# A stick-breaking attention layer whose input arrives transposed, with the token scale multiplied in after the projections

## The chip, the core and the metric

The kernel runs as one program on one core of a Trainium2 chip. The metric is the device time of one execution in microseconds; lower is better. The kernel before takes 697.34 us (median of 3 runs, 697.03 to 698.51).

The engines are named as in the profile: PE is TensorE, PEld its weight loads, DVE VectorE, ACT ScalarE, POOL GpSimd, SP SyncE (which here only starts transfers).

## The reference

With DEPTH = 1 only layer 0 is computed: a pre-norm, stick-breaking attention with a SiLU gate, a residual, and a final norm. x is 1024 tokens by 1024 features, float32.

```
h = x * rsqrt(mean(x*x, -1) + eps) * norm_g         # per token scale, per feature gain
q, k, v, gate = split(h @ w_in, 4)                  # 1024 x 4096, 16 heads of 64
z = q k^T / 8, masked to key < query                # per head
log_beta = log_sigmoid(z); log_1m = log_beta - z
a = exp(log_beta + sum of log_1m over later keys)
o = a v;  y = x + (o * silu(gate)) @ w_out
out = y * rsqrt(mean(y*y, -1) + eps) * final_g
```

## The kernel before

Every matrix product is made in three float32r products of high and low parts (hi times hi, hi times lo, lo times hi). `hT` holds h by features: hi and lo, 8 feature blocks of 128, 1024 tokens. `half` 0 and 1 are tokens 0 to 511 and 512 to 1023. A weight unit is the 1024 x 128 slice of w_in for one kind (k, v, q or gate) and one pair of heads; one unit on one half is 24 matmuls of 128x512 into one PSUM bank.

The order of work is written out by hand, one in-order stream for each engine, with semaphores between them.

**The prologue.** x is loaded by tokens, in 8 blocks of 128 tokens (512 KB each). ACT and DVE sum the squares of each block, a root and one Newton step give `rstd` (one number for each token), and DVE and ACT multiply the blocks by it (`scale_x`). PE then transposes the scaled blocks into PSUM (`transpose_x`, 16 times four 128x128 transposes), ACT writes the hi part with the gain (`hi_x`), DVE the lo part (`lo_x`). Among them stand the six projections that pair 0 needs, in the order k0, v0, k1, v1, q0, q1 (kind and half), in two PSUM banks. ACT evicts each bank to the buffer `stage` (`to_stage`, a copy); DVE splits k and q into heads (`heads_hi`, `heads_lo`); v is transposed by PE and split. `z` below is the first scores matmul, the end of the prologue.

**The pairs.** Eight pairs of heads follow (p = 0 to 7), 16 slots each (s = 0 to 15, eight query blocks of rising width, 128 to 1024 keys, for each head). In a slot PE makes the scores of this query block into `z_ps`, half of a projection for the next pair into the one bank `proj_ps`, the products of a with v for the slot before, and the transposes of a. ACT makes two sigmoids from the scores (`rest` and the beta values). DVE runs the scan over `rest` (L1016), whose length is the width of the block. POOL multiplies beta by the scanned row (L1115), makes the lo parts of the weights (L1091) and multiplies o by the gate (L1103). `evac_at` puts one eviction of `proj_ps` at the head of every even slot: k in slots 2 and 4, v in 6 and 8, q in 10 and 12, the gate in 14 and in slot 0 of the next pair. ACT does it before. PE's next projection waits for it (one bank), and in slots 6 and 8 so do PE's transposes of v (L495).

**The last pair and the tail.** Pair 7 has only gate projections (evicted in slots 0, 4 and 8), beside them the output projection begins; then come the output projection, the residual and the final norm.

## Time and profile before

| | us |
|---|---|
| median of 3 runs | 697.34 |
| the profiled execution, its own time | 696.88 |
| its span | 694.8 |
| PE busy | 670.2 (96%) |
| DVE busy | 481.4 (69%) |
| ACT busy | 426.4 (61%) |
| POOL busy | 282.0 (41%) |

The time of the profiled execution is 2.1 us more than its span. A row of the timeline gives the start, the duration, the engine, the line and operation, the output and inputs, how many instructions are merged in it, and in square brackets how long the engine had been idle before it and who ended that.

### The profile page before, as it was taken

The numbers are of one execution on the slowest core, as the hardware profiler recorded it, in microseconds if no ns is written. First come the engines' busy times: TensorE is split into PE (matmuls) and PEld (weight loads), VectorE is DVE, ScalarE is ACT, GpSimd is POOL, SyncE is SP. The second block draws the span as 40 slices with busy tenths as digits, with TensorE's granted clock in tenths as the row PEclk, the third lists the DMA queues.
The fourth block names the chain that finished last, engine by engine and source line by source line (L and its number), as shares of the span: only waits on it lengthen the run. The fifth ranks groups of instructions, "written<-read, shape, count | busy, mean of one in ns | idle before, by whom it ended". The sixth has DMA issues, their size and how long they took to land.

```text
span 694.8 us, 10872 instructions
## 1 busy us (share of the span) xinstructions
PE 670.2 (96%) x3426; PEld 563.4 (81%) x3426; DVE 481.4 (69%) x636; ACT 426.4 (61%) x795; POOL 282.0 (41%) x225
## 2 busy tenths in 40 slices
PE   5999999999999999999999999999999997999995
PEld 4787888888888888888888888888888776888884
DVE  5835666776678677867776677667766798735565
ACT  5614767676767676767676767666766675622333
POOL 2122434453545445444554454435353543315100
PEclk9999999999999999999999999999999999999999
DMA  7131301241114110410042014201420148523332
GB/s 288 46 95 43 92 31 31 61 122 33 31 51 131 31 33 33 136 44 20 25 129 67 16 32 121 76 15 30 121 60 30 61 137 290 211 92 94 125 145 92
DMA packets 28122, 57.64 MB, mean 83 GB/s; under 512 B 3376, under 2 KB 3376, under 8 KB 28080
## 3 DMA queue, kind: packets, MB, share of 16 engines
q1 hardware_dynamic: 25312, 51.13, 24.0%
q10 hardware_dynamic: 2736, 6.03, 2.3%
q8 instruction: 16, 0.26, 0.2%
q14 instruction: 26, 0.21, 0.1%
q0 software_dynamic: 32, 0.00, 0.0%
HBM read 37.23 MB, written 11.53 MB: 70 GB/s over the span
## 4 chain that ended last, share of the span: by engine, by line
PE 90%; DVE 5%; ACT 2%; DMA 1%; POOL 1%; issue 1%; ACTq 0%; DVEq 0%; POOLq 0%
PE proj_ps L486 46%; PE o_ps L632 10%; PE z_ps L581 9%; PE t_ps L644 9%; PE z_ps L561 8%; PE proj_ps L561 4%; PE o_ps L486 2%; DVE rest L1016 2%; PE t_ps L495 1%; DMA a_group<-x 1%; DVE gate L982 1%; ACT stage L719 1%; PE z_ps L506 1%; DVE arena L314 0%; DVE aT L1000 0%
## 5 line engine op out<-in xcount | busy, mean ns | idle before, releaser
L486 PE MATMUL proj_ps<-hT,w_split 128*128 128x512 f32 x1464 | 359.9, 394 | 2.2 <-DVE hT L889 1.4
L486 PEld LDWEIGHTS proj_ps<-hT,w_split 128*128 128x128 f32 x1464 | 270.0, 188 | 57.6 <-DVE hT L889 2.3
L1115 POOL TENSOR_TENSOR a_group<-a_group,rest 128x128 f32<-128x128 f32 (+7 forms) x128 | 158.0, 1235 | 300.0 <-DVE rest L1016 300.0
L1016 DVE TENSOR_TENSOR_SCAN rest<-rest,restart 128x128 f32<-128x128 f32 (+7 forms) x128 | 203.6, 1591 | 16.0 <-ACT rest L809 15.5
L1000 DVE TENSOR_TENSOR aT<-t_ps,aT 128x512 fp32r<-128x512 f32 (+2 forms) x160 | 93.1, 607 | 35.1 <-ACT aT L794 33.6
L794 ACT ACTIVATE aT<-t_ps 128x512 fp32r<-128x512 f32 (+2 forms) x160 | 80.2, 532 | 59.2 <-PE t_ps L644 57.6
L1091 POOL TENSOR_TENSOR w_split<-w_raw,w_split 128x512 fp32r<-128x512 f32 x64 | 91.7, 1434 | 38.1 <-DVE w_split L851 38.1
L581 PE MATMUL z_ps<-arena 128*128 128x512 f32 (+2 forms) x384 | 96.3, 366 | 0.3 <-DVE arena L938 0.3
L938 DVE TENSOR_TENSOR arena<-stage,arena 64x512 fp32r<-64x512 f32 x64 | 44.0, 687 | 67.9 <-ACT arena L739 67.3
L809 ACT ACTIVATE rest<-z_ps 128x128 f32<-128x128 f32 (+7 forms) x128 | 83.9, 655 | 8.9 <-PE z_ps L581 8.6
L644 PE MATMUL t_ps<-ident,a_group 128*128 128x128 f32 x576 | 84.6, 274 | 0.4 <-POOL a_group L1115 0.4
L811 ACT ACTIVATE a_group<-z_ps 128x128 f32<-128x128 f32 (+7 forms) x128 | 84.4, 659 | 0.0
L632 PE MATMUL o_ps<-aT,arena 128*128 128x512 f32 (+2 forms) x320 | 82.7, 364 | 1.7 <-DVE aT L1000 1.7
L644 PEld LDWEIGHTS t_ps<-ident,a_group 128*128 128x128 f32 x576 | 70.0, 142 | 8.5 <-issue 0.6
L719 ACT ACTIVATE stage<-proj_ps 128x512 f32<-128x512 f32 x61 | 36.5, 598 | 61.3 <-PE proj_ps L486 61.3
L632 PEld LDWEIGHTS o_ps<-aT,arena 128*128 128x128 f32 x320 | 59.5, 188 | 16.6 <-DVE aT L1000 4.2
L581 PEld LDWEIGHTS z_ps<-arena 128*128 128x128 f32 x384 | 59.6, 190 | 5.2 <-DVE arena L938 0.8
L561 PE MATMUL z_ps<-arena,hT 128*128 128x512 f32 x246 | 57.7, 391 | 0.0
L786 ACT ACTIVATE oT<-o_ps 64x512 f32<-64x512 f32 x32 | 19.0, 593 | 62.2 <-PE o_ps L632 62.2
L561 PEld LDWEIGHTS z_ps<-arena,hT 128*128 128x128 f32 x246 | 45.8, 188 | 9.4
L990 DVE TENSOR_TENSOR oT<-o_ps,oT 64x512 f32<-64x512 f32 x32 | 22.0, 689 | 25.6 <-ACT oT L786 25.3
L746 ACT ACTIVATE w_split<-w_raw 128x512 fp32r<-128x512 f32 x56 | 35.9, 641 | 0.6
(86 smaller groups left out, 460.7 us busy)
## 6 DMA issues: line engine op xcount, KB each, us to landing
w_raw<-w_in SPq DMA_DIRECT2D x64, 256.0 KB, 2.6
arena<-arena SPq DMA_DIRECT2D x32, 256.0 KB, 4.3
wo_raw<-w_out SPq DMA_DIRECT2D x16, 256.0 KB, 3.8
o_hi_scratch<-o_split SPq DMA_DIRECT2D x14, 256.0 KB, 2.1
o_lo_scratch<-o_split SPq DMA_DIRECT2D x14, 256.0 KB, 2.4
hT<-o_hi_scratch SPq DMA_DIRECT2D x14, 256.0 KB, 4.9
hT<-o_lo_scratch SPq DMA_DIRECT2D x14, 256.0 KB, 6.0
a_group<-x SPq DMA_DIRECT2D x14, 256.0 KB, 3.6
```

The lines of the kernel that those rows point to most:

```text
L486: mm = nc.tensor.matmul(bank[:, :], w_split[:, ring, wl, b, :], hT[:, hl, b, half * HALF:(half + 1) * HALF], start=(b == 0 and n == 0), st ...
L561: mm = nc.tensor.matmul(bank[:, :], hT[:, ol, b, tokens], w_out_of(nh, wl)[:, b, :], start=(b == first and m == 0), stop=(b == last and m ...
L581: mm = nc.tensor.matmul(z[:, c0:c1], q, k_of(par, hh, swapped)[:, c0 - first:c1 - first], start=not swapped, stop=swapped)
L632: mm = nc.tensor.matmul(o_ps[:, c:HALF], v_of(apar)[:, j, 2 * ahh:2 * ahh + 2, :] .rearrange("p x d -> p (x d)"), moving, start=(j == 0 an ...
L644: last = nc.tensor.transpose(t_ps[t % 2][:, i2 * P:(i2 + 1) * P], a_g[grp][:, i2, j * P:(j + 1) * P], ident[:, :])
L794: nc.scalar.activation(to, t_ps[t % 2][:, rel * P:HALF], ACT.Copy).then_inc(t_hi, 1)
L809: nc.scalar.activation(rest[:, s % 2, S - width:S], z_ps[s % 2][:, first:first + width], ACT.Sigmoid, scale=-SCALE).then_inc(rest_ready, 1)
L811: nc.scalar.activation(a_g[grp][:, i % GQ, 0:width], z_ps[s % 2][:, first:first + width], ACT.Sigmoid, scale=SCALE).then_inc(beta_ready, 1)
L1000: nc.vector.tensor_tensor(lo, t_ps[t % 2][:, rel * P:HALF], hi.bitcast(F32), ALU.subtract).then_inc(t_lo, 1)
L1016: nc.vector.tensor_tensor_scan(span, span, restart[:, S - 1:(S - 1 - width if width < S else None):-1], 0.0, ALU.mult, ALU.max).then_inc(s ...
L1091: nc.gpsimd.tensor_tensor(to[:, 1], w_raw[:, part, :].rearrange("p (b n) -> p b n", b=4), to[:, 0].bitcast(F32), ALU.subtract).then_inc(w_ ...
L1115: nc.gpsimd.tensor_tensor(a, a, rest[:, s % 2, S + 1 - width:S + 1], ALU.mult).then_inc(a_ready, 1)
```

## The change

x is handed to the kernel a second time, by features (`x_t`, transposed on the host), and loaded in 16 tiles of 128 features by 512 tokens. ACT and DVE split each tile into hi and lo with the gain, straight from SBUF and without the token scale. The token scale commutes with the projection, so it is multiplied in when a projection is evicted: `to_stage` is now DVE's, one tensor_tensor of the PSUM bank with `token_scale`, a 128x1024 tile that has the scale of each token in all partitions. To make it, ACT squares the 16 tiles, POOL adds the squares over the 8 feature blocks of each half (7 adds for each half, 128x512), PE sums them over the partitions with a column of ones, the root and the Newton step follow as before, PE transposes the broadcast result, and ACT copies it to SBUF. DVE, not POOL, makes the lo parts of the first four weight tiles. The prologue's projections have six banks instead of two; the warm-up is 12 transposes instead of 34. The a matrix is stored as a triangle to make room, and the residual's x tiles go to other buffers.

```diff
@@ buffers
+        token_scale = sb("token_scale", [P, S])
+        ones = sb("ones", [P, 1])
+        def x_raw(n):
+            return x_cols[:, n // KB, n % KB, :]
+        squares = [oT[:, 0:HALF], oT[:, HALF:S], gate[:, 0:HALF], gate[:, HALF:S]]
+        first_banks = [proj_ps, o_ps] + z_banks
@@ PE
-            def transpose_x(n):
-                half, b = n // KB, n % KB
-                wait(pe, xt_lo, n - 3)
-                for i in range(4):
-                    ...
-                last.then_inc(xt_done, 1)
+            def sum_squares(half):
+                pe.wait_ge(squares_added, (KB - 1) * (half + 1))
+                for i in range(GQ):
+                    last = nc.tensor.matmul(t_ps[half][:, i:i + 1], rest[:, half, i * P:(i + 1) * P], ones[:, :],
+                                            start=True, stop=True)
+                last.then_inc(ssq_done, 1)
+            def spread_scale(half):
+                pe.wait_ge(rstd_ready, 5 * half + 5)
+                ...
+                    last = nc.tensor.transpose(t_ps[half][:, i * P:(i + 1) * P],
+                                               rstd[:, b:b + 1].to_broadcast([P, P]), ident[:, :])
             for h, (kind, half) in enumerate(PROLOGUE):
                 unit = "kvq".index(kind)
-                wait(pe, stage_ready, h - 1)
+                if h == 4:
+                    transpose_v(0, 0, 1, 1)
                 for b in range(KB):
                     pe.wait_ge(xt_lo, KB * half + b + 1)
                     pe.wait_ge(w_ready, 2 * unit + b // 4 + 1)
-                    mm = project(unit % 2, (proj_ps, o_ps)[h % 2], half, b)
+                    mm = project(unit % 2, first_banks[h], half, b)
+                    if b == 3 and h == 2:
+                        spread_scale(0)
+                    if b == 3 and h == 3:
+                        sum_squares(1)
+                if h == 1:
+                    sum_squares(0)
+                if h == 3:
+                    spread_scale(1)
@@ ACT
+HI_THEN_SQUARES = (0, 0, 1, 0, 1, 0, 1, 4, 0, 1, 0, 1, 0, 1, 0, 1)
+            for n in range(2 * KB):
+                hi_x(n)
+                for _ in range(HI_THEN_SQUARES[n]):
+                    square_x(squared)
+                    squared += 1
+                if n == KB + 4:
+                    root(slice(0, GQ), t_ps[0][:, 0:GQ], ssq_done, 1)
+            scale_half(0)
+            while squared < 2 * KB:
+                ...
-            def to_stage(bank, h, buf):
-                act.wait_ge(proj_done, h + 1)
-                nc.scalar.activation(stage[:, buf, :], bank[:, :], ACT.Copy).then_inc(stage_ready, 1)
@@ DVE
-                nc.vector.scalar_tensor_tensor(hT[:, 1, b, cols], z_banks[n % 4][:, :], g_col[:, b:b + 1],
+                nc.vector.scalar_tensor_tensor(hT[:, 1, b, cols], x_raw(n), g_col[:, b:b + 1],
                                                hT[:, 0, b, cols].bitcast(F32), ALU.mult, ALU.subtract
+            def to_stage(bank, h, half, buf):
+                dve.wait_ge(proj_done, h + 1)
+                nc.vector.tensor_tensor(stage[:, buf, :], bank[:, :], token_scale[:, half * HALF:(half + 1) * HALF],
+                                        ALU.mult).then_inc(stage_ready, 1)
@@ DVE, slot()
                 if evac:
                     kind, half, h = evac
+                    ...
+                    to_stage(proj_ps, h, half, half)
@@ POOL
-            for n in range(2 * UNITS0 + 2):
+            for half in range(2):
+                for b in range(1, KB):
+                    add_square(half, b)
+            for n in range(4, 2 * UNITS0 + 2):
                 lo_w(n, (n // 2) % 2, n % 2)
```

The first of three places is DVE in slots 5 to 8 of pair 0, before; the later pairs have the same order, with the split of o (`o_split`) in slots 2 and 6 besides. The scan is listed as SCALAR_TENSOR_TENSOR on `rest`; its width tells the slot.

```order
L1016 SCALAR_TENSOR_TENSOR rest<-rest,restart 128x768 [waits rest_ready]
L1000 TENSOR_TENSOR aT<-t_ps,aT 128x384 [waits t_hi]
L1016 SCALAR_TENSOR_TENSOR rest<-rest,restart 128x896 [waits rest_ready]
L945 TENSOR_TENSOR arena<-t_ps,arena 128x4x128 [waits t_hi]
L1000 TENSOR_TENSOR aT<-t_ps,aT 128x256 [waits t_hi]
L1016 SCALAR_TENSOR_TENSOR rest<-rest,restart 128x1024 [waits rest_ready]
L1000 TENSOR_TENSOR aT_pad<-t_ps,aT_pad 128x128 [waits t_hi]
```

The same place after:

```order
L1022 SCALAR_TENSOR_TENSOR rest<-rest,restart 128x768 [waits rest_ready]
L917 TENSOR_TENSOR stage<-proj_ps,token_scale 128x512 [waits proj_done,qk_split]
L1006 TENSOR_TENSOR aT<-t_ps,aT 128x384 [waits t_hi]
L1022 SCALAR_TENSOR_TENSOR rest<-rest,restart 128x896 [waits rest_ready]
L902 TENSOR_TENSOR arena<-t_ps,arena 128x4x128 [waits t_hi]
L1006 TENSOR_TENSOR aT<-t_ps,aT 128x256 [waits t_hi]
L1022 SCALAR_TENSOR_TENSOR rest<-rest,restart 128x1024 [waits rest_ready]
L917 TENSOR_TENSOR stage<-proj_ps,token_scale 128x512 [waits proj_done,qk_split]
L1006 TENSOR_TENSOR aT_pad<-t_ps,aT_pad 128x128 [waits t_hi]
```

Both evictions of v now stand on DVE behind the scan of the slot before.

The second place is DVE in the prologue after, up to the first eviction; `hT<-x_cols` is `lo_x`, `w_split` rows are the split of the weights.

```order
L851 CAST w_split<-w_raw 128x512 [waits w_loaded0,g_loaded]
L911 TENSOR_TENSOR w_split<-w_raw,w_split 128x512 [waits w_hi]
L879 SCALAR_TENSOR_TENSOR hT<-x_cols,g_col,hT 128x512 [waits xt_hi] x3
L851 CAST w_split<-w_raw 128x512 [waits w_loaded1]
L911 TENSOR_TENSOR w_split<-w_raw,w_split 128x512 [waits w_hi]
L879 SCALAR_TENSOR_TENSOR hT<-x_cols,g_col,hT 128x512 [waits xt_hi] x5
L851 CAST w_split<-w_raw 128x512 [waits w_loaded0]
L911 TENSOR_TENSOR w_split<-w_raw,w_split 128x512 [waits w_hi]
```

All of these read SBUF only; before, `lo_x` read `z_ps`, and POOL did the subtraction for the weights.

The third place is PE around the sum of squares after: the end of v0 (bank `o_ps`), the four sums, and the start of k1.

```order
L499 MATMUL o_ps<-hT,w_split 128x512 x2
L517 MATMUL t_ps<-ones,rest 128x1 [waits squares_added]
L517 MATMUL t_ps<-ones,rest 128x1 x3
L499 MATMUL z_ps<-hT,w_split 128x512 [waits w_ready,xt_lo]
L499 MATMUL z_ps<-hT,w_split 128x512 x2
```

PE's projections of k1 stand behind a wait for POOL's first seven adds; the same four sums stand again in the middle of v1, behind a wait for all fourteen.

## Rows read from the trace of the kernel before

**Rows 1.** The page: busy time of each engine, and the chain by engine.

```profile
PE 670.2 (96%) x3426; PEld 563.4 (81%) x3426; DVE 481.4 (69%) x636; ACT 426.4 (61%) x795; POOL 282.0 (41%) x225
PE 90%; DVE 5%; ACT 2%; DMA 1%; POOL 1%; issue 1%; ACTq 0%; DVEq 0%; POOLq 0%
```

**Rows 2.** Windows: us, busy by engine, PEclk (granted clock), DMA share, GB/s.

```profile
200.00:271.00 71.00, 71.00 (x371) 60.21 (x371) 50.98 (x59) 48.60 (x91) 33.54 (x27) 1.00 0.20 61
...
580.00:584.00 4.00, 3.68 (x15) 3.45 (x16) 3.07 (x7) 2.33 (x6) 0.71 (x1) 0.59 0.96 298
```

**Rows 3.** Groups by line, 0 to 60 us; columns as on the page.

```profile
L1091 POOL TENSOR_TENSOR w_split<-w_raw,w_split 128x512 fp32r<-128x512 f32 x8 | 10.4, 1314 | 38.1 <-DVE w_split L851 38.1
L506 PE MATMUL z_ps<-ident,a_group 128*128 128x128 f32 x48 | 7.8, 274 | 0.5 <-DVE a_group L882 0.3
```

**Rows 4.** Timeline of the prologue.

```profile
4.13 0.20 ACT L671 ACTIVATE newton<-eps_col 128x1 f32<-128x1 f32 x1
...
5.54 1.23 DVE L877 CUSTOM_DVE_ANT_0 gate<-a_group 128x1024 f32<-128x1024 f32 x1 [4.38 <-DMA a_group<-x]
...
9.62 0.30 ACT L667 ACTIVATE rstd<-ssq,eps_col 128x4 f32<-128x4 f32 x1
...
10.83 0.16 DVE L868 TENSOR_TENSOR rstd<-rstd,newton 128x4 f32<-128x4 f32 x1
...
50.56 5.74 PE L486 MATMUL o_ps<-hT,w_split 128*128 128x512 f32 x24
...
59.36 0.73 PE L581 MATMUL z_ps<-arena 128*128 128x256 f32 x4 [0.34 <-DVE arena L938]
```

**Rows 5.** Timeline, slots 5 to 8 of pair 5.

```profile
429.13 2.75 DVE L1016 TENSOR_TENSOR_SCAN rest<-rest,restart 128x768 f32<-128x768 f32 x1
...
432.43 0.60 PE L495 MATMUL t_ps<-ident,stage 128*128 128x128 f32 x4
...
437.30 1.78 POOL L1115 TENSOR_TENSOR a_group<-a_group,rest 128x896 f32<-128x896 f32 x1 [2.02 <-DVE rest L1016]
...
437.66 0.41 DVE L1000 TENSOR_TENSOR aT<-t_ps,aT 128x256 fp32r<-128x256 f32 x1
438.38 2.85 DVE L1016 TENSOR_TENSOR_SCAN rest<-rest,restart 128x1024 f32<-128x1024 f32 x1 [0.31 <-ACT rest L809]
...
440.03 0.60 ACT L719 ACTIVATE stage<-proj_ps 128x512 f32<-128x512 f32 x1 [0.78 <-PE proj_ps L486]
...
440.69 0.66 PE L495 MATMUL t_ps<-ident,stage 128*128 128x128 f32 x4
```

**Rows 6.** Timeline, slot 15 and the next pair's slot 0: scan, PE's next projection.

```profile
473.59 2.29 DVE L1016 TENSOR_TENSOR_SCAN rest<-rest,restart 128x1024 f32<-128x1024 f32 x1 [1.08 <-ACT rest L809]
...
475.93 3.03 PE L486 MATMUL proj_ps<-hT,w_split 128*128 128x512 f32 x12
```

**Rows 7.** Timeline, POOL and DVE right after that.

```profile
476.03 2.00 POOL L1115 TENSOR_TENSOR a_group<-a_group,rest 128x1024 f32<-128x1024 f32 x1 [2.33 <-DVE rest L1016]
...
476.65 1.93 DVE L982 TENSOR_TENSOR gate<-stage,gate 128x512 f32<-128x512 f32 x1 [0.77 <-ACT gate L776]
...
477.98 1.74 POOL L1091 TENSOR_TENSOR w_split<-w_raw,w_split 128x512 fp32r<-128x512 f32 x1
...
478.70 1.30 DVE L1016 TENSOR_TENSOR_SCAN rest<-rest,restart 128x128 f32<-128x128 f32 x1
```

**Rows 8.** Timeline, slot 2 of pair 5: splits on ACT and DVE.

```profile
413.00 1.27 ACT L739 ACTIVATE arena<-stage 64x512 fp32r<-64x512 f32 x2
...
414.30 1.39 DVE L938 TENSOR_TENSOR arena<-stage,arena 64x512 fp32r<-64x512 f32 x2 [2.24 <-ACT arena L739]
...
415.72 1.29 DVE L1000 TENSOR_TENSOR aT<-t_ps,aT 128x512 fp32r<-128x512 f32 x2
...
416.93 0.68 DVE L1006 TENSOR_TENSOR o_split<-oT,o_split 128x512 fp32r<-128x512 f32 x1
```

**Rows 9.** Timeline, PE in the last pair.

```profile
580.32 0.79 PE L632 MATMUL o_ps<-aT_pad,arena 128*128 128x256 f32 x2 [4.16 <-DVE aT_pad L1000]
```

More of the change, by code:

```diff
@@ L378, in _ @@
                 load_w(n, n % 2, n % 2, kinds[n // 2] * KB)
-                if n == 1:
-                    for b in (5, 7):
+                if n < 2:
+                    for b in range(4 * n + 1, 4 * n + 5, 2):
+                        load_x_block(sp, b)
+                if n == 3:
+                    for b in range(KB, 2 * KB):
                         load_x_block(sp, b)
@@ L660, in _, with root @@
         def _(act):
+            act.dma_start(g_col[:, :], norm_g).then_inc(g_loaded, 16)
             for b in range(0, KB, 2):
                 load_x_block(act, b)
-            act.wait_ge(consts_ready, 2)
-            def root(cols, ready, count):
+            act.wait_ge(eps_ready, 1)
+            def root(cols, sums, ready, count):
                 act.wait_ge(ready, count)
-                nc.scalar.activation(rstd[:, cols], ssq[:, cols], ACT.Sqrt, scale=1.0 / D,
+                nc.scalar.activation(rstd[:, cols], sums, ACT.Sqrt, scale=1.0 / D,
@@ L688, in _, with scale_half @@
-            act.wait_ge(x_squared_dve, 2)
-            root(slice(0, 4), x_squared, 2)
-            square_x(2, 4)
-            def scale_x(blocks):
-                for b in blocks:
-                    nc.scalar.activation(x_blocks[b], x_blocks[b], ACT.Copy, scale=rstd[:, b:b + 1]
-                                         ).then_inc(x_scaled_act, 1)
-            act.wait_ge(rstd_ready, 5)
-            scale_x(X_ACT[:1])
+            def scale_half(half):
+                act.wait_ge(scale_done, half + 1)
+                nc.scalar.activation(token_scale[:, half * HALF:(half + 1) * HALF], t_ps[half][:, :], ACT.Copy
+                                     ).then_inc(scale_ready, 1)
@@ L738, in heads_hi @@
                     to = q_of(par, hh) if kind == "q" else k_of(par, hh, False)
-                    last = nc.scalar.activation(to[rows, cols], stage[rows, half, :], ACT.Copy)
+                    last = nc.scalar.activation(to[rows, cols], stage[rows, buf, :], ACT.Copy)
                 last.then_inc(qk_hi, 1)
+            for h, (kind, half) in enumerate(PROLOGUE):
+                if kind in "kq":
+                    act.wait_ge(stage_ready, h + 1)
+                    heads_hi(kind, 0, half, 0 if kind == "k" else half)
+                if h == 0:
+                    root(slice(GQ, KB), t_ps[1][:, 0:GQ], ssq_done, 2)
+                    scale_half(1)
+                if h in (3, 5):
+                    v_hi(0, h // 2 - 1, h // 2 - 1, h // 2 - 1)
             def split_hi_w(ring, part, unit):
@@ L950, in _, with split_w @@
+            def split_w(n):
+                next_w(n)
+                lo_w(n)
+            dve.wait_ge(g_loaded, 16)
+            split_w(0)
+            for n in range(KB):
+                lo_x(n)
+                if n == 2:
+                    split_w(1)
+            split_w(2)
+            split_w(3)
             for n in range(KB, 2 * KB):
+                if n == KB + 5:
+                    dve.wait_ge(table_loaded, 1)
+                    dve.wait_ge(root_ready, 1)
+                    rsqrt(slice(0, GQ), t_ps[0][:, 0:GQ], 0)
@@ new lines, in _ @@
+                if h in (3, 5):
+                    dve.wait_ge(t_done, h // 2)
+                to_stage(first_banks[h], h, half, h % 2)
+                if kind in "kq":
+                    heads_lo(kind, 0, half, h % 2, {0: 1, 2: 2, 4: 3, 5: 4}[h])
+                if h == 1:
+                    for n in (4, 5):
+                        dve.wait_ge(proj_done, 3)
+                        next_w(n)
+                    dve.wait_ge(root_ready, 2)
+                    rsqrt(slice(GQ, KB), t_ps[1][:, 0:GQ], 1)
@@ L1092, in lo_w, with add_square @@
                                         to[:, 0].bitcast(F32), ALU.subtract).then_inc(w_ready, 1)
-            for n in range(2 * UNITS0 + 2):
+            def add_square(half, b):
+                n = KB * half + b
+                pool.wait_ge(x_squared, n + 1)
+                total = rest[:, half, 0:HALF]
+                other = squares[(n - 1) % 4] if b == 1 else total
+                if b > 1:
+                    pool.wait_ge(squares_added, (KB - 1) * half + b - 1)
+                nc.gpsimd.tensor_tensor(total, other, squares[n % 4], ALU.add).then_inc(squares_added, 1)
+            for half in range(2):
+                for b in range(1, KB):
+                    add_square(half, b)
+            for n in range(4, 2 * UNITS0 + 2):
                 lo_w(n, (n // 2) % 2, n % 2)
```

219 lines of the change are left out of this document (78 added, 141 removed).

## The prediction

> **What bounds the kernel now.** I read the page first: PE is busy 96% of the span and carries 90% of the chain that ended last [rows 1]. The windows then say where it is not: a pair in the middle has PE busy for all of its 71 us, with DVE at 51, ACT at 49 and POOL at 34 [rows 2]. So a microsecond taken from PE is a gain, and a microsecond by which another engine lets PE wait is a loss, for in the middle nothing gives it back. Last I read the timeline at two places: the prologue, which ends at 59.36 us with the first scores matmul [rows 4], and the slots in which `proj_ps` is evicted [rows 5, 6].
>
> **The change removes** 64 transposes of 128x128 from PE in the prologue: 48 take 7.8 us [rows 3], so 64 take 10.4 us. It also removes the order "squares, root, scale, transpose, split" ahead of the first projection. Were PE the only limit, the prologue would be about 10 us shorter.
>
> **What now sets the prologue.** One rule of this machine decides it, and the trace shows it. A DVE instruction with two inputs in SBUF and a POOL instruction with inputs in SBUF do not run together. POOL's L1115 runs 476.03 to 478.03; DVE's gate product, asked for at 476.65, ends at 478.58, 0.55 us after POOL. POOL's L1091, asked for at 477.98, ends at 479.72, 1.14 us after DVE; and the short scan, asked for at 478.70, ends 0.28 us after that [rows 7]. They wait in full, and take turns. A DVE instruction with one input in PSUM doesn't wait: the 256-wide L1000 takes 0.41 us in the middle of POOL's L1115 [rows 5]. The Trainium skill says the same in "SBUF — State Buffer" (section "SBUF: two separate sides": the port pair of the two is an exclusive lock held for a whole instruction), and by it the change is worse than its list of operations. Were it a sharing of bandwidth, the first rival's sum below would hold.
>
> Before, `lo_x` read PSUM. Now it reads two SBUF tiles while POOL adds squares. Step by step, all times from the span's start:
>
> - First data: two 512 KB blocks had landed by 5.54 us [rows 4]; the first tile and the first weights are half of that and are there by about 4.2 (an estimate from that row). ACT was free at 4.33 [rows 4] and now issues one more transfer (some 0.5 us): first hi ends at 5.5, first lo at 6.2, and PE starts there. ACT's order puts the second square at 9.2, and POOL's first add runs 9.2 to 10.5 (1.31 us each alone [rows 3]).
> - From there DVE and POOL take turns, 0.54 + 1.17 = 1.7 us each time [rows 7], where DVE alone would take 0.68 [rows 8]. Five `lo_x` and four adds: the last tile of half 0 is ready at 10.5 + 5 x 0.54 + 4 x 1.17 = 17.9. Then the third weight tile (two DVE steps, with adds 6 and 7 between them) at 21.0, the fourth at 22.0. k0 ends at 18.6, v0 (24 matmuls, 5.5 us by 5.74 with the last one's tail [rows 4]) at 26.5, the four sums at 26.9.
> - Root and Newton step take 1.4 us (9.62 to 10.99 [rows 4]): 28.4. The remaining `lo_x` and the adds 8 to 14 follow in turns, with two head splits of k0 among them: 29.05 + 5 x 1.17 + 2 x 1.29 + 2 x 0.54 + 2 x 0.58 = 39.7.
> - PE has k1 done at 33.2, half of v1 at 35.95, and waits there for add 14: 39.8, a wait of 3.8 us. Then the sums 0.4, the second half 2.7, the scale's transposes 0.5, those of v 0.6: q0 starts at 44.0, q1 ends at 55.0. The lo weights of q (POOL, at 42.8) are just in time; so is the swap of k's halves, which is issued near 48.
> - After q1: transposes of v 0.6, eviction 0.6, head split 1.27 on ACT and 1.39 on DVE [rows 8]: `z` at 59.0. Before it is 59.36. The gain is 0.4 us where 10 were on offer.
>
> To this I add the clock. After PE had waited 4.16 us [rows 9], its granted clock was 0.59 in the next 4 us [rows 2], that is mostly the lower of its two levels, 1.2 GHz: (1 - 0.59) x 4 = 1.6 us lost. The new wait of 3.8 us is of that size. The Trainium skill ("TensorE: Matmul & The Clock Gate", Part 1) has the clock fall to half after idling, and the trace agrees. **Prologue: -0.4 + 1.6 = +1.2 us.** Its bounds are -9.5 (no turns) and +5 (below).
>
> **The eviction in the pairs.** 0.6 us leaves ACT, and about the same comes to DVE: reading a PSUM bank and one SBUF tile, the second of two L1000 adds 1.29 - 0.69 = 0.60 us [rows 8]. DVE has the time; what counts is where it stands in DVE's order, which is behind the scan of the slot before, and PE waits for it.
>
> - Slot 6: the scan of 768 ends at 431.88, the eviction at 432.48. PE's transposes of v run from 432.43, with their first load some 0.2 ahead [rows 5]: 0.3 us late.
> - Slot 8: the scan of 1024 ends at 441.23, the eviction would end at 441.83. ACT's ended at 440.63, and PE's transposes came at once [rows 5]. 1.2 us late. The 0.3 us of slot 6 come off, since this scan's end is set by POOL's L1115 (end 439.08, plus 2.15) and not by PE. Both slots: 1.2 us.
> - Slot 0: the scan ends at 475.88, the eviction at 476.48; PE's next projection stood at 475.93 [rows 6]. 0.6 us.
> - Slots 2, 4, 10, 12 and 14: the scan before is short or done before the projection is. In slot 2 DVE waited 2.24 us for ACT's head split [rows 8], so the eviction fits in that wait. Behind it, ACT's head split starts 0.1 us later, and PE isn't touched. Cost nothing; without that cover each would be 0.6.
>
> What queues behind the late eviction: on PE everything of the slot (it is in order); on ACT the head split or the sigmoid of the gate; on DVE nothing that wasn't waiting for PE anyhow. Since PE is busy all the time [rows 2], 1.8 us per pair stay. Pairs 1 to 6: 10.8. Pair 0 has no gating work on POOL ahead of its scans; I take one stall of 0.6. In the last pair DVE is itself late (PE waits 4.16 us for it [rows 9]), and two gate evictions of 0.6 stand in its chain: 1.2. **Pairs: +12.6 us.** Bounds: nothing, if PE were not held at these slots, and 16.5, if the scan of slot 15 too had a POOL instruction ahead of it as that of slot 7 has (0.56 more, 2.85 against 2.29 [rows 5, 6]), in seven pairs.
>
> The rest costs nothing: transfers of x for the residual go to other buffers at the same point of SP's queue, the triangle has the same rows for the same instructions, the 256 KB transfers replace the 512 KB ones, and the shorter warm-up lies ahead of the first data. SP now issues eight x tiles between the weights of v and of q, but they are wanted only from 14 us on.
>
> **Sum.** +1.2 + 12.6 = +13.8 us on the profiled execution's own 696.9 us gives 710.7. That execution is 0.5 us below the median of the three runs, so I write 711.
>
> **Rivals.**
> - *The turns don't hold in the prologue* (lock for this form of DVE instruction absent, or POOL gives way). For it: no row shows a scalar_tensor_tensor with both tiles in SBUF beside POOL. Against it: tensor_tensor and the scan both wait [rows 7]. Then half 0 is split at 12.5, v0 ends at 19.1, POOL's adds are back to back and end at 30.6, and `z` comes at 49.9: -9.5, no long wait and no clock loss. 696.9 - 9.5 + 12.6 = 700.
> - *The clock is low in k0 and v0 too.* For it: PE works only 0.7 of each 1.7 us there and then waits 2.4 us, and rows 2 show what a wait does. Against it: none of these gaps is as long as the wait of rows 9. v0 delays the sums, and by them everything to `z`: up to +3.7 us more, 715.
> - *Faster: PE is not held at slots 6, 8 and 0.* The place is DVE's queue at the eviction, the price the 11.4 us of pairs 0 to 6. It needs the wide scans to end before the projection does. For it: a scan without POOL ahead is 0.56 us shorter (2.29 against 2.85 [rows 5, 6]), and DVE's total has room [rows 2]. Against it: in slot 8 the scan starts when ACT's sigmoid ends [rows 5], and that starts with PE's scores, so even 2.29 us would end at 440.67 and the eviction 0.6 after ACT's. Then only the prologue and the last pair count: 696.9 + 1.2 + 1.2 = 699 with my prologue, 689 with the first rival's, and it is faster from the point where the prologue gives more than the pairs take. As one case I put it at 693.
> - *The change doesn't do what it says*: only where the eviction waits for `token_scale`; after the prologue that is set once and is no wait.
>
> **Chances.** My forecast 0.62 (706 to 715); no turns 0.15 (697 to 703); low clock in k0 and v0 0.12 (713 to 718); PE not held 0.11 (687 to 699). The range of 8 in 10 is 699 to 717: it takes in most of the second case and leaves out the last. What a measurement of this kernel can tell from no change is about 0.2%, 1.4 us. Faster by more than that: 0.11, from the last case and the lower edge of the second. Within it: 0.04. Slower: 0.85.
>
> **What would show it.** The first scores matmul at 59 to 61 us (50 would be the first rival). POOL's adds and DVE's `lo_x` alternating, with `lo_x` shown at 1.7 us instead of 0.7. PE waiting for POOL's last add near 36 to 40 us, with a granted clock well under 1 behind it. In each pair PE waiting for DVE's `stage` in slots 8 and 0, together 1.8 us, and each pair longer by that. DVE busy up by about 36 us in the pairs, ACT down by as much. If PE shows no waits in the middle, the forecast is wrong by 12 us; if `lo_x` stays at 0.7 us while POOL adds, it is wrong by 10.

## The result, and the profile after

| | before | after |
|---|---|---|
| median, us | 697.18 (696.77 to 698.51, 4 runs) | 716.06 (715.09 to 716.97, 4 runs) |
| span of the profiled execution | 694.8 | 715.2 |
| first scores matmul (`z`) | 59.36 | 64.84 |
| pair 0, from `z` to the end of its last scan | 63.14 | 64.96 |
| pairs 1 to 6, each | 70.67 | 72.77 |
| last pair | 61.82 | 62.58 |
| rest | 86.4 | 86.1 |

The change makes the kernel slower: ratio 1.0265 [1.0253, 1.0277]. A pair is measured here from the end of one scan of slot 15 to the next. The 20.4 us of span are 5.5 of the prologue, 1.8 of pair 0, 12.6 of pairs 1 to 6, 0.8 of the last, less 0.3.

The page of after, busy time and chain by engine, as [rows 1]:

```profile
PE 679.5 (95%) x3364; PEld 562.1 (79%) x3364; DVE 526.1 (74%) x686; ACT 394.8 (55%) x744; POOL 295.4 (41%) x234
PE 81%; DVE 7%; issue 5%; ACT 3%; POOL 2%; DMA 1%; DVEq 0%; ACTq 0%; POOLq 0%
```

PE has 62 instructions less than before and is busy 9.3 us longer; DVE gained 44.7 us, ACT lost 31.6. PE's share of the chain fell from 90% to 81%: it now waits. In a middle pair DVE is at 56.4 us where it was at 51.0, and ACT at 43.7 where it was at 48.4; over seven pairs that is 37 and 33 us, where about 36 was named for each.

The timeline of the prologue of after, filtered to DVE, then to POOL, then to PE (L879 is `lo_x`, L1106 POOL's add, L517 the sums over the partitions):

```profile
10.51 7.55 DVE L879 SCALAR_TENSOR_TENSOR hT<-x_cols,g_col,hT 128x512 fp32r<-128x512 f32 x5
...
23.23 3.39 DVE L879 SCALAR_TENSOR_TENSOR hT<-x_cols,g_col,hT 128x512 fp32r<-128x512 f32 x5
...
12.83 2.98 POOL L1106 TENSOR_TENSOR rest<-rest,gate 128x512 f32<-128x512 f32 x2 [0.43 <-ACT gate L700]
...
40.00 3.21 POOL L1106 TENSOR_TENSOR rest<-rest,gate 128x512 f32<-128x512 f32 x2
...
18.12 0.97 PE L499 MATMUL proj_ps<-hT,w_split 128*128 128x512 f32 x3 [0.74 <-DVE hT L879]
21.32 8.37 PE L499 MATMUL o_ps<-hT,w_split 128*128 128x512 f32 x24 [2.23 <-DVE w_split L911]
29.52 0.95 PE L517 MATMUL t_ps<-ones,rest 128*128 128x1 f32 x8
...
43.27 1.26 PE L517 MATMUL t_ps<-ones,rest 128*128 128x1 f32 x8 [2.18 <-POOL rest L1106]
...
64.84 0.74 PE L601 MATMUL z_ps<-arena 128*128 128x256 f32 x4 [0.77 <-DVE arena L895]
```

With POOL beside them five `lo_x` take 7.55 us; with POOL idle five take 3.39. But v0's 24 matmuls take 8.37 us where such 24 took 5.74 before [rows 4]. The windows say why (us, busy PE, PEld, DVE, ACT, POOL, granted clock, DMA):

```profile
15.00:20.00 5.00, 2.61 (x9) 1.17 (x8) 4.96 (x4) 4.40 (x8) 4.57 (x4) 1.00 0.81 284
20.00:25.00 5.00, 3.69 (x9) 2.94 (x10) 4.97 (x6) 0.33 (x1) 2.15 (x2) 0.51 0.26 81
25.00:30.00 5.00, 5.00 (x23) 4.06 (x21) 1.62 (x3) 0.00 (x0) 0.00 (x0) 0.81 0.07 27
...
40.00:45.00 5.00, 2.82 (x15) 2.19 (x14) 3.93 (x7) 0.26 (x1) 4.49 (x4) 0.90 0.00 0
45.00:50.00 5.00, 5.00 (x23) 4.13 (x22) 1.67 (x7) 0.60 (x1) 1.20 (x1) 0.76 0.41 105
```

PE was busy 2.6 of 5 us, and then its clock was 0.51, nearly all at 1.2 GHz. By the clock column 0.49 x 5 + 0.19 x 5 = 3.4 us are lost around v0, of which 2.6 show in v0's own 8.37 us, and 0.10 x 5 + 0.24 x 5 = 1.7 in v1.

The timeline of after, slots 6 and 8 of a middle pair and slot 0 of the last, as [rows 5, 6]; L917 is the eviction, L508 the transposes of v:

```profile
372.63 2.82 DVE L1022 TENSOR_TENSOR_SCAN rest<-rest,restart 128x768 f32<-128x768 f32 x1
...
375.38 0.66 DVE L917 TENSOR_TENSOR stage<-proj_ps,token_scale 128x512 f32<-128x512 f32 x1
...
376.09 0.66 PE L508 MATMUL t_ps<-ident,stage 128*128 128x128 f32 x4
...
382.16 2.63 DVE L1022 TENSOR_TENSOR_SCAN rest<-rest,restart 128x1024 f32<-128x1024 f32 x1 [0.52 <-ACT rest L809]
...
384.71 0.66 DVE L917 TENSOR_TENSOR stage<-proj_ps,token_scale 128x512 f32<-128x512 f32 x1
...
385.43 0.66 PE L508 MATMUL t_ps<-ident,stage 128*128 128x128 f32 x4 [0.75 <-DVE stage L917]
...
567.16 1.62 PE L499 MATMUL proj_ps<-hT,w_split 128*128 128x512 f32 x6 [0.49 <-DVE stage L917]
```

Each eviction starts when the scan ahead of it ends, and PE stands behind it. In slot 6 PE's transposes start at 376.09, right after the eviction's end at 376.04, and yet no idle time of PE is listed: the matmul before them was still running. Their weight load had waited 0.27 us for DVE's `stage`.

One thing was in no forecast. PE's projections of one pair, by windows filtered to `proj_ps` (busy PE, then clock), before and after:

```profile
193.00:263.63 70.63, 46.99 (x192) 1.00 0.20 61
```

```profile
202.50:275.20 72.70, 47.79 (x192) 1.00 0.20 59
```

The same 192 matmuls at the same clock take 0.80 us more. Taken over pairs 1 to 6, one starts 231.7 ns after the other before and 235.5 after, though the matmul and the sizes of its operands are the same.

### The profile page after: what moved, and what is told of

Same layout as the page of the kernel before. It is cut to its first block, busy times and chain, and to the rows that moved or that the text cites. A ratio compares the mean times of both kernels' runs of the same rounds, so it can differ in the third digit from the quotient of the medians.

```text
span 715.2 us, 10802 instructions
## 1 busy us (share of the span) xinstructions
PE 679.5 (95%) x3364; PEld 562.1 (79%) x3364; DVE 526.1 (74%) x686; ACT 394.8 (55%) x744; POOL 295.4 (41%) x234
## 4 chain that ended last, share of the span: by engine, by line
PE 81%; DVE 7%; issue 5%; ACT 3%; POOL 2%; DMA 1%; DVEq 0%; ACTq 0%; POOLq 0%
PE proj_ps L499 39%; PE o_ps L652 9%; PE t_ps L664 8%; PE z_ps L601 8%; PE z_ps L581 8%; PE proj_ps L581 4%; PE z_ps L499 2%; ACT rest L809 2%; DVE stage L917 2%; DVE rest L1022 2%; PE t_ps L508 1%; POOL rest L1106 1%; PE o_ps L499 1%; DVE hT L879 1%; DMA x_cols<-x_t 1%
## 5 line engine op out<-in xcount | busy, mean ns | idle before, releaser
L499 PEld LDWEIGHTS proj_ps<-hT,w_split 128*128 128x128 f32 x1416 | 262.8, 189 | 69.8 <-DVE hT L879 8.0
L1132 POOL TENSOR_TENSOR a_tri<-a_tri,rest 128x128 f32<-128x128 f32 (+7 forms) x128 | 156.7, 1225 | 313.8 <-DVE rest L1022 300.0
L1022 DVE TENSOR_TENSOR_SCAN rest<-rest,restart 128x128 f32<-128x128 f32 (+7 forms) x128 | 209.9, 1641 | 17.2 <-ACT rest L809 16.5
L1095 POOL TENSOR_TENSOR w_split<-w_raw,w_split 128x512 fp32r<-128x512 f32 x60 | 87.1, 1452 | 8.7 <-DVE w_split L851 8.7
L664 PE MATMUL t_ps<-ident,a_tri 128*128 128x128 f32 x576 | 84.5, 274 | 0.4 <-POOL a_tri L1132 0.4
L811 ACT ACTIVATE a_tri<-z_ps 128x128 f32<-128x128 f32 (+7 forms) x128 | 84.3, 659 | 0.0
L895 DVE TENSOR_TENSOR arena<-stage,arena 64x512 fp32r<-64x512 f32 x64 | 45.4, 710 | 43.2 <-ACT arena L740 42.8
L664 PEld LDWEIGHTS t_ps<-ident,a_tri 128*128 128x128 f32 x576 | 69.9, 141 | 8.3 <-issue 0.6
L740 ACT ACTIVATE arena<-stage 64x512 fp32r<-64x512 f32 x64 | 40.3, 630 | 64.1 <-DVE stage L917 63.7
L917 DVE TENSOR_TENSOR stage<-proj_ps,token_scale 128x512 f32<-128x512 f32 x59 | 40.1, 680 | 16.1 <-PE proj_ps L499 16.1
```

Of the source, the lines that this page charges most:

```text
L499: mm = nc.tensor.matmul(bank[:, :], w_split[:, ring, wl, b, :], hT[:, hl, b, half * HALF:(half + 1) * HALF], start=(b == 0 and n == 0), st ...
L664: last = nc.tensor.transpose(t_ps[t % 2][:, i2 * P:(i2 + 1) * P], a_of(GQ * grp + i2)[:, j * P:(j + 1) * P], ident[:, :])
L811: nc.scalar.activation(a_of(i), z_ps[s % 2][:, first:first + width], ACT.Sigmoid, scale=SCALE).then_inc(beta_ready, 1)
L1022: nc.vector.tensor_tensor_scan(span, span, restart[:, S - 1:(S - 1 - width if width < S else None):-1], 0.0, ALU.mult, ALU.max).then_inc(s ...
L1095: nc.gpsimd.tensor_tensor(to[:, 1], w_raw[:, part, :].rearrange("p (b n) -> p b n", b=4), to[:, 0].bitcast(F32), ALU.subtract).then_inc(w_ ...
L1132: nc.gpsimd.tensor_tensor(a, a, rest[:, s % 2, S + 1 - width:S + 1], ALU.mult).then_inc(a_ready, 1)
```

## The experiments

The sums below use three numbers of each profiled execution: `z`, the middle pair (mean of pairs 1 to 6), and the time.

| | us (median) | ratio to before | `z` | pair 0 | middle pair |
|---|---|---|---|---|---|
| e1_act_evicts | 707.59 | 1.0136 [1.0118, 1.0155] | 65.92 | 63.74 | 71.20 (one 72.45) |
| e2_before_dve_evicts | 708.19 | 1.0153 [1.0136, 1.0170] | 59.42 | 63.90 | 72.39 |
| e3_thin_adds | 703.29 | 1.0081 [1.0064, 1.0097] | 52.34 | 64.95 | 72.77 |
| e4_layout | 713.16 | 1.0213 [1.0192, 1.0234] | 64.61 | 63.96 | 72.38 |
| e5_dve_adds | 709.75 | 1.0179 [1.0162, 1.0196] | 55.77 | 66.47 | 72.79 |
| e6_v_unscaled | 709.77 | 1.0175 [1.0158, 1.0192] | 60.95 | 63.97 | 71.70 |
| e7_room32 | 717.85 | 1.0291 [1.0274, 1.0308] | 62.86 | 65.04 | 72.87 |
| e8_warm | 712.88 | 1.0217 [1.0200, 1.0235] | 61.13 | 64.95 | 72.76 |
| e9_w_place | 712.24 | 1.0218 [1.0197, 1.0238] | 59.50 | 63.95 | 72.43 |
| e10_best | 699.24 | 1.0020 [1.0008, 1.0032] | 55.59 | 65.95 | 71.30 |
| e11_best_gate | 701.60 | 1.0054 [1.0038, 1.0070] | 57.58 | 63.38 | 71.26 (one 72.58) |
| e12_best_order | 698.54 | 1.0026 [1.0000, 1.0051] | 52.91 | 64.94 | 71.23 (one 76.31) |

The prologues of e1, e4, e6, e7 and e9 have the changed kernel's instructions in its order (e6 leaves the token factor out of two evictions of v; e4, e7 and e9 have tensors at other places), and yet their `z` differ by 6.4 us. With it goes the granted clock. In e6 and e9 it is 1.00 in every 5 us up to 55 us; here is e6 where after had 0.51, and then e9 there and in the 5 us before:

```profile
20.00:25.00 5.00, 3.47 (x15) 2.87 (x16) 4.96 (x6) 0.00 (x0) 2.38 (x2) 1.00 0.26 55
```

```profile
15.00:20.00 5.00, 1.93 (x6) 0.97 (x6) 4.97 (x4) 3.85 (x7) 4.42 (x5) 1.00 0.69 245
20.00:25.00 5.00, 4.48 (x20) 3.76 (x21) 4.97 (x7) 0.00 (x0) 1.51 (x1) 1.00 0.36 105
```

In e9 PE was busy for less of the 5 us than in after (1.93 against 2.61), and its clock did not fall. The timed runs show the same spread: the mean granted clock of e9's four was 0.994, 0.991, 0.986 and 0.986, and their times 708.7, 710.9, 713.9 and 713.6. All four of after were between 0.986 and 0.989. So `z` of one execution has a spread of its own, and the middle pair is the safer number.

### Eviction and layout, two by two

```diff
@@ e1: ACT, slot()
+                    act.wait_ge(proj_done, h + 1)
+                    nc.scalar.activation(stage[:, half, :], proj_ps[:, :], ACT.Copy).then_inc(stage_ready, 1)
@@ e2: DVE, slot() of the kernel before
+                    dve.wait_ge(proj_done, h + 1)
+                    nc.vector.tensor_scalar(stage[:, half, :], proj_ps[:, :], 1.0, None, ALU.mult
+                                            ).then_inc(stage_ready, 1)
@@ e4
-        ones = sb("ones", [P, 1])
+        ones = sb("ones", [P, HALF])[:, 0:1]
```

> The changed kernel with the evictions of the pairs back on ACT, as a plain copy (the token factor is left out of all projections of the pairs; the prologue is as changed). Theory: the 14.9 us that the pairs lost are PE's waits for DVE's late eviction in slots 6, 8 and 0, about 1.25 us per pair, plus a second term of 0.8 us per pair that I had not forecast, a projection matmul taking 235.3 ns from start to start instead of 231.1. If that second term also comes from DVE's eviction, all of it goes: pitch 231, pairs of 70.65 us, z still at 64.8, time about 701. If it comes from where the tensors now lie in SBUF, only the waits go: pitch 235, pairs of 71.5, time about 707. If neither theory holds and the pairs lose their time elsewhere, it stays near 716.

> The kernel before with one edit: the evictions of the pairs are moved from ACT to DVE, at the place in DVE's order that they have in the changed kernel (multiplied by the constant 1.0, so nothing is left out). Prologue and tensors stay as before. Theory of the late eviction: PE waits about 1.25 us per pair for DVE's stage. With the slower matmuls caused by DVE's eviction: pitch 235, pairs of 72.8, time 697.2 + 14 = 711. With the slower matmuls caused by the tensors' places: pitch 231, pairs of 72.0, 697.2 + 9 = 706. If eviction by DVE costs nothing and the pairs lost their time otherwise: 697.

> The changed kernel with one tensor made larger: the one-column tile of ones gets 512 columns of room, of which only the first is used. With that rest, aT, stage, w_split and all the tensors behind it in SBUF lie at exactly the addresses that they have in the kernel before, instead of 2044 bytes lower. If the 4 ns of each projection matmul come from the place of the weights (w_split) in SBUF: pitch back to 231, 0.8 us less in each pair, time about 709 to 710. If they come from DVE's eviction: pitch 235, time 716.

PE's waits in e2 (us in total, times, longest):

```profile
PE t_ps L495 <- DVE stage L975: 5.8, 7, 0.9
PE proj_ps L486 <- DVE stage L975: 4.2, 9, 0.6
```

PE busy with `proj_ps` in one middle pair, of e1, of e2 and of e4:

```profile
200.75:271.95 71.20, 47.76 (x192) 1.00 0.20 60
```

```profile
195.60:268.00 72.40, 47.04 (x192) 1.00 0.21 59
```

```profile
200.80:273.20 72.40, 47.00 (x192) 1.00 0.21 59
```

The middle pair is 70.67 us (ACT evicts, old places), 72.39 and 72.38 (DVE evicts, old places: e2 and e4), 71.20 (ACT, new places), 72.77 (DVE, new places). Late eviction costs 1.72 us at the old places and 1.57 at the new; the places cost 0.53 and 0.39. The slower matmuls follow the places and not the eviction. e4's pair fell by 0.39 us where 0.8 was named, and its time was 3 us above 709 to 710: the projections came back to 231.7 ns and PE spent 0.79 us less of a pair on them, but the 512-wide matmuls of aT went from 229.5 to 234.6 ns (0.24 us more with `o_ps`), and PE, busy 71.02 us of the pair and not 71.62, was idle 0.2 us longer. e2 came out 2 us above its 706 because a pair lost 1.72 and not 1.25: I had added up the waits that the trace lists, and such a one as in slot 6 above is not among them.

### Which tensor it is

```diff
@@ e7 (8) and e9 (504), ahead of w_split
         eps_col = sb("eps_col", [P, 1])
+        sb("room", [P, 8])
```

> The changed kernel with 32 bytes of unused room ahead of w_split, and nothing else. In the kernel before, w_split began at a multiple of 64 bytes in SBUF and aT 32 bytes off one; in the changed kernel it is the other way round. From start to start a projection matmul (weights from w_split) took 231.7 ns before and 235.5 after, a matmul of aT against v 234.6 before and 229.5 after. Theory: a tensor that begins 32 bytes off a multiple of 64 makes PE's reads of it slower. Then the projection matmuls take 231.7 again and those of aT stay at 229.5: 192 x 3.8 ns = 0.7 us less per pair, pairs of 72.05, 710 to 711 in all. If it is the distance from other tensors, or the 2016 bytes by which w_split moved, the projection stays at 235.5 and the time at 716.

> The changed kernel with 2016 bytes of unused room ahead of w_split, so that w_split alone lies again where it lay before; every other tensor stays where the change put it. Moving it by 32 bytes left the projection matmuls at 235.7 ns from start to start; moving it together with all tensors behind the ones by 2016 bytes gave 231.7, and slowed the matmuls of aT from 229.5 to 234.6. Theory one, it is w_split's own place that counts for the projection: 231.7 for it, 229.5 still for aT, pairs of 72.05 us, 710 to 711. Theory two, it is the place of another tensor that moved (rest, aT, stage, the identity) or the distance to it: 235.5 for the projection, 716.

PE busy with `proj_ps` in one middle pair, e7, then e9:

```profile
200.70:273.50 72.80, 47.83 (x192) 1.00 0.21 59
```

```profile
195.70:268.10 72.40, 47.05 (x192) 1.00 0.20 59
```

e7's theory falls: moved by 32 bytes, the projection stays at 235.7 ns from start to start. In e9 w_split alone is back at its old place, and it is 232.0. So w_split's place sets it (only `wo_raw`, which shares its room and which PE never reads, moved with it). But the 512-wide matmuls of aT, which did not move in either, went from 229.5 to 232.3 in e7 and to 235.0 in e9. A pair of e9 was 72.43 us and not the 72.05 that was named, and its time 712.24 and not 710 to 711. What in w_split's address does this stays open; no rule is shown, only that three addresses give three pairs of figures.

### The prologue

```diff
@@ e3: POOL
-                nc.gpsimd.tensor_tensor(total, other, squares[n % 4], ALU.add)
+                nc.gpsimd.tensor_tensor(total[:, 0:8], other[:, 0:8], squares[n % 4][:, 0:8], ALU.add)
@@ e8: PE
+                    if h == 0:
+                        keep_warm(5)
                     pe.wait_ge(xt_lo, KB * half + b + 1)
@@ e5: the adds on DVE
+                nc.vector.tensor_tensor(total, other, squares[n % 4], ALU.add).then_inc(squares_added, 1)
```

> The changed kernel with POOL's 14 adds of squares cut from 512 to 8 columns, in the same order and with the same waits (the sum of squares is left out for all but 8 columns). Theory of the turns: lo_x falls from 1.2 to 1.5 us to 0.68 everywhere, half 0 is split by about 14 us instead of 18, PE waits neither for POOL nor long for DVE, and z comes at 52 to 54 instead of 64.84: time about 716 - 11 = 705. If the turns cost little and the prologue is held by the landing of x or by the low clock: z at 62 or later, 713 to 716. The pairs stay at 72.8 us either way.

> The changed kernel with identity transposes of no use put where PE waits in the prologue: 5 ahead of each feature tile of k0, 18 ahead of v0, 16 ahead of the second sum of squares (0.11 us each at full clock). Theory: part of the late z is the clock. In the changed kernel it was at half for about 6.8 us in k0 and v0 and 3.4 us in the second half of v1, 5 us of loss. If work without use keeps it up, these go: z at 60 to 62, time 711 to 713. If the turns alone set the chain (PE's low clock being hidden by its waits for the next tile), z stays at 64 to 65; and if the transposes come in the way of the tiles, z is at 66 or later.

> The changed kernel with the 14 adds of squares moved from POOL to DVE, after all of lo_x, and the order of the prologue behind them arranged to fit (ACT makes hi of all 16 tiles first; the sums and the spreading of the token factor come one half projection later on PE; v0's eviction goes ahead of k0's head split). Nothing is left out. Theory of the turns: with POOL out of the way lo_x takes 0.68 us, PE never waits long in the prologue, its clock stays at full, and the adds (14 x 0.67 = 9.4 us) fit into DVE's free time after 20 us: z at 49 to 53 instead of 64.8, time 701 to 704. If DVE is too full behind 25 us, the late evictions move z to 56 or more, and 708 or more. If adds of two SBUF tiles on DVE held ACT or PE up as well, z would be near 60.

The timeline of e3, `lo_x` and PE's first projections:

```profile
10.46 2.74 DVE L879 SCALAR_TENSOR_TENSOR hT<-x_cols,g_col,hT 128x512 fp32r<-128x512 f32 x4
...
7.73 8.55 PE L499 MATMUL proj_ps<-hT,w_split 128*128 128x512 f32 x24 [3.37 <-DVE hT L879]
16.11 5.76 PE L499 MATMUL o_ps<-hT,w_split 128*128 128x512 f32 x24
```

e3 shows the turns: with POOL's adds shortened and nothing else taken from DVE, `lo_x` is at 0.68 us from start to start again, k0 (once its tiles are there) and v0 run through, and `z` is 12.5 us earlier, all at full clock. Its median is 12.8 us below that of after. e8 shows the clock apart from the turns: its `lo_x` mean is that of after (1202 ns both, 748 in e3), and its v0 took 5.85 us and not 8.37. Here is the group of `lo_x` in e8, and from its timeline v0:

```profile
L888 DVE SCALAR_TENSOR_TENSOR hT<-x_cols,g_col,hT 128x512 fp32r<-128x512 f32 x16 | 18.4, 1202 | 2.5 <-ACT hT L714 2.5
```

```profile
21.67 5.85 PE L499 MATMUL o_ps<-hT,w_split 128*128 128x512 f32 x24
```

`z` is 3.7 us earlier than in after, and all four timed runs had a mean clock of 0.991 to 0.994, where after's had 0.986 to 0.989. e6 and e9 come to the same or lower without filling (60.95 and 59.50), but only in some executions. The turns at full clock cost the rest: 61.1 less 52.3, 8.8 us, or 7.2 by e9. e5 removes the turns without leaving anything out, but has its q0 and q1 chain in series at the end. PE waited there (timeline), and the clock was 0.66 in the next window:

```profile
55.77 1.12 PE L600 MATMUL z_ps<-arena 128*128 128x256 f32 x4 [4.36 <-DVE arena L895]
```

```profile
55.00:60.00 5.00, 4.23 (x14) 3.52 (x15) 2.47 (x5) 2.92 (x6) 1.18 (x2) 0.66 0.08 31
```

So `z` missed its 49 to 53 by 2.8 us, pair 0 took 1.5 us more, and the time missed 701 to 704 by 6.

### One place of the late eviction

```diff
@@ e6: ACT evicts v unscaled; its factor goes into the split of aT
-                    nc.scalar.activation(to, t_ps[t % 2][:, rel * P:HALF], ACT.Copy).then_inc(t_hi, 1)
+                    nc.scalar.activation(to, t_ps[t % 2][:, rel * P:HALF], ACT.Copy,
+                                         scale=rstd[:, j:j + 1]).then_inc(t_hi, 1)
```

> The changed kernel with v's evictions in the pairs back on ACT as plain copies, and v's token factor multiplied in elsewhere: at the split of the transposed weights aT, whose partitions are v's tokens, as the per-partition scale of ACT's copy and of DVE's subtraction. The number of instructions stays as it is; nothing is left out. Theory of the late eviction, place by place: PE's waits for DVE's stage in slots 6 and 8 (the transposes of v) go, that of slot 0 stays: 1.2 us less per pair, pairs of 71.5 to 71.6, 707 to 708 in all. If the loss came from DVE's added work as such and not from these two places, only the 1.3 us of DVE time would count: 714. If the scaled forms take longer than the plain ones on ACT or DVE (0.1 us each, 24 per pair), it gives part of this back: 709 to 712.

The pair fell by 1.07 us, and 1.2 was named; 1.57 of eviction less 1.07 leaves 0.5 for slot 0. The median missed 707 to 708 by 2 us. About 1 of these is the smaller gain in seven pairs. The last pair, where DVE is late by itself, grew by 0.9; the scaled forms are longer (512 wide, means of both traces: ACT 687 against 597 ns, DVE 748 against 688), and I put it down to them without a run of its own. The Trainium skill has the ACT part in "ScalarE: Activation LUTs" (section "What ACT_TABLE_LOAD costs": "each `[128,1]` pointer operand adds" about 93 ns); the 90 ns agree.

### A better version

```diff
@@ e10: e5 + e6 + e4, WARM_UP 40, no POOL read in the prologue, v0 and v1 evicted by ACT
@@ e11: slot 0 on ACT too
+                        nc.vector.tensor_tensor(stage[:, 1, :], stage[:, 1, :], token_scale[:, HALF:S], ALU.mult
+                                                ).then_inc(g_scaled, 1)
@@ e12: e10, prologue's end reordered
-            heads_lo("q", 0, 0, 0, 3)
             evict(5)
+            heads_lo("q", 0, 0, 0, 3)
```

> A version meant to beat both: the changed kernel with the adds of squares on DVE, the lo weights of the prologue on DVE too (POOL reads nothing there), 28 more warming transposes at the start, v evicted unscaled by ACT in the prologue and in the pairs with its token factor in the split of aT, and the tensors at their places of the kernel before. Nothing is left out. By the parts measured so far: z at 51 to 52 us (PE without a wait from 9 us on; 55.6 before with a serial end of 4.4 us that this order takes away), against 59.4 in the kernel before; pair 0 at 63.7, pairs 1 to 6 at 71.7 - 0.4 = 71.3 each (70.67 before), last pair 63.4 (61.8 before), tail 86.1: 691 to 692 + 2 = 693 to 694, by 4 us faster than the kernel before. The rival: that the order of the prologue is again held up somewhere (DVE full, a low clock), with z at 55 or more: 697 or more.

> As e10_best, and the eviction of slot 0 (the gate's second half) is done by ACT as a plain copy as well; DVE multiplies the token factor into stage in place afterwards, ahead of the sigmoid. Theory of the late eviction: PE's wait of 0.6 us in slot 0 goes, 7 times: pairs of 70.7, 4 us less than e10_best, 689 to 690. Rival: the multiplication has two inputs in SBUF and so takes turns with POOL, which multiplies in slot 0 too; it comes up to 1.2 us later, delays the sigmoid, the gate product and DVE's split behind it, and the pairs stay at 71.3 or grow: no better than e10_best.

> e10_best with the end of its prologue in another order, nothing left out: the sums and spreads of the token factor stand where their inputs are ready (the sums of half 0 in the second half projection of half 1, its spread at the start of q0, those of half 1 late in q0 and early in q1), ACT takes the second root ahead of v's split, DVE evicts q1 ahead of q0's head split, and 18 identity transposes fill PE's last wait ahead of z. In e10_best PE waited 1.2 + 1.2 us for sums and root, then 3.2 us ahead of z at 55.45, and its clock was at half behind that wait: pair 0 took 65.95 us where e11_best_gate had 63.38. Theory: these waits are the order's, so z comes at 51 to 52 and pair 0 takes 63.4; with pairs of 71.3, a last pair of 63.2 and a tail of 86.1 the time is 692 to 694.5, faster than the kernel before by 3 to 5 us. Rival: the fill only moves the wait (the chain eviction, head split, swap of k sets z at 54 or more): 696 to 698, no difference from before.

e10's middle pair is the 71.3 that was named, but PE waited 3.17 us ahead of `z` at 55.59, and pair 0 then took 65.95. It is no faster than before. e11 waited as long ahead of its `z`, but its clock stayed up and pair 0 took 63.38. Here are the first scores matmul and a window with the clock behind it, of e10, then of e11:

```profile
55.59 1.22 PE L611 MATMUL z_ps<-arena 128*128 128x256 f32 x4 [3.17 <-DVE arena L923]
55.00:60.00 5.00, 4.41 (x12) 3.67 (x13) 1.60 (x3) 2.91 (x6) 1.25 (x3) 0.50 0.01 4
```

```profile
57.58 0.74 PE L612 MATMUL z_ps<-arena 128*128 128x256 f32 x4 [3.16 <-DVE arena L926]
60.00:65.00 5.00, 4.49 (x20) 3.49 (x19) 3.33 (x6) 3.86 (x8) 2.51 (x3) 1.00 0.17 52
```

e11's pairs stayed at 71.3 as its rival said: the new multiplication (L1036) has two SBUF inputs. In the usual pair it starts just ahead of POOL's product and takes 0.69 us; POOL's then takes 2.49 instead of 2.00, the gate product behind it (L1047) waits for POOL in turn, and PE waits 0.38 us for `aT_pad` in place of the 0.5 for `stage`. This is the start of pair 3:

```profile
263.58 0.69 DVE L1036 TENSOR_TENSOR stage<-stage,token_scale 128x512 f32<-128x512 f32 x1
263.64 2.49 POOL L1178 TENSOR_TENSOR a_tri<-a_tri,rest 128x1024 f32<-128x1024 f32 x1 [2.29 <-DVE rest L1081]
...
267.00 0.51 PE L663 MATMUL o_ps<-aT_pad,arena 128*128 128x256 f32 x2 [0.38 <-DVE aT_pad L1065]
```

In pair 5 alone POOL was first, by 0.02 us. It runs 406.10 to 408.10, and DVE ends 0.54 us after it, as in [rows 7]; PE's wait is 1.44, and this pair is the 72.58 of the table. That order went with a pair 1.3 us longer, 1.06 of it in PE's wait.

```profile
406.10 2.00 POOL L1178 TENSOR_TENSOR a_tri<-a_tri,rest 128x1024 f32<-128x1024 f32 x1 [2.29 <-DVE rest L1081]
406.12 2.52 DVE L1036 TENSOR_TENSOR stage<-stage,token_scale 128x512 f32<-128x512 f32 x1 [0.17 <-ACT stage L795]
...
410.64 0.51 PE L663 MATMUL o_ps<-aT_pad,arena 128*128 128x256 f32 x2 [1.44 <-DVE aT_pad L1065]
```

e12 brought `z` to 52.9 where 51 to 52 was named, but pair 0 took 64.94 and not 63.4, behind a wait of 2.18 us ahead of `z` and 0.89 and 0.77 of the clock. Its runs spread from 696.1 to 704.8. The profiled one has, at the start of pair 3, where the loop over pairs turns back, a gap that nothing in the trace ends, and 0.83 of the clock behind it:

```profile
262.68 1.21 PE L610 MATMUL z_ps<-arena 128*128 128x256 f32 x4 [2.73 <-issue]
```

```profile
260.00:280.00 20.00, 17.32 (x78) 14.57 (x79) 10.55 (x16) 9.26 (x20) 7.85 (x7) 0.83 0.07 26
```

That pair took 76.31 us, 5 more than its neighbours. e1's one long pair (72.45) is pair 3 as well, and ACT has such a gap of 1.41 us at its start:

```profile
273.53 0.63 ACT L787 ACTIVATE gate<-stage 128x512 f32<-128x512 f32 x1 [1.41 <-issue]
```

What makes the gap is not known. Without it e12's profiled execution would have taken some 696 us (700.95 less 5.1, an estimate), which is where its fastest runs are. No version beat the kernel before: e12's interval touches no change.

## Why the prediction was right, and where it was off

711 was forecast, within 699 to 717 and slower with 0.85; 716.06 came. It lies above the 706 to 715 of the forecast's own case, in the 713 to 718 that the second rival had with a chance of 0.12. It took that rival and a term that stood nowhere to get there. By its own steps, on the span (+13.8 forecast, +20.4 measured):

- **The turns of DVE and POOL** held as read from [rows 7]. v0 was to start at 21.0 and did at 21.32; e3 shows that the turns are the cause. That the last tile of half 0 was ready at 18.06, with 17.9 forecast, is in part luck: POOL's first add began at 11.10 and not at 9.2, and in exchange a tile took 1.51 us and not 1.71 (the sum had 1.17 us for POOL's turn, where the rows read beside it give 1.14). Without them `z` is at 52.3, where the first rival had 49.9.
- **The clock** was mis-sized. The forecast gave it 1.6 us, behind the wait for POOL only. In the profiled execution of after it was low around v0 as well, as the second rival said: v0 took 2.6 us longer for it, and POOL's last add ended at 43.2 and not 39.7. Where the clock stayed full, the forecast's 59.0 without a clock term is near: in e9 the last add ended at 39.7 and `z` came at 59.50, in e6 at 60.95. So the prologue is +0.1 and +1.6 in these two, and +5.5 in the profiled execution of after, where +1.2 stood. The argument against the rival, that none of the gaps is as long as that of [rows 9], was wrong: PE was busy 2.6 of 5 us, waits of 0.7 us among them, and the clock fell.
- **The wait for POOL's last add** was 2.2 us in after, e6 and e9 alike, and not 3.8, since k1 had itself waited 1.2 us for `lo_x`. Behind it the clock fell in after (0.90, then 0.76) and not in e6 or e9, so the 1.6 us that the forecast put there are not sure either.
- **The eviction in the pairs**: 1.8 us per pair forecast, 1.72 measured by e2 and 1.57 by e1 against after. e6 takes the v slots away and gets 1.07 where 1.2 stood. The last pair gave 0.8 where 1.2 stood. Over all pairs e2 less before is 0.8 + 6 x 1.72 + 0.8 = 11.9, forecast 12.6; the medians differ by 10.8.
- **"The rest costs nothing"** failed: moving w_split by 2016 bytes made the projections slower, 1.0 us in pair 0 and 0.4 in each of pairs 1 to 6 (after against e4, and e9 the same), some 3.3 us in all, where the forecast had a term of nothing for everything that moved. Nothing in the trace of before could show it.
- **PE not held at slots 6, 8, 0**, the faster rival, fell: the waits stand in the trace, and taking them away gives the time back.

The Trainium skill's lock ("SBUF — State Buffer", section "SBUF: two separate sides") agrees with e3 and e11. Its clock rule ("TensorE: Matmul & The Clock Gate", Part 1), a clock that follows how busy PE has been, leaves room for the fall behind k0, which my comparison of single waits did not. It does not tell when: e9 kept its clock at 1.00 with PE busy 1.93 of 5 us, and e11 behind a wait of 3.16 us, where e10 lost it behind 3.17. What decides between them is not shown.

## What to carry to other kernels

Removing work from the busiest engine pays nothing when what replaces it moves onto an engine that stands late in that engine's chain: look for the instruction that the eviction queues behind, and count the wait once per pass of the loop. An operation that read PSUM and now reads two SBUF tiles beside a busy POOL costs 1.5 us and not 0.7, and the gaps that this tears into PE's work can cost more through its clock (3.7 us here, beside 7 to 9 of the turns). And when a change moves buffers, compare the start-to-start time of matmuls that nobody touched.
